# A hybrid layer's mixers reordered: a head's inputs prepared while its neighbour runs, the first phase's products in another order

## The reference

```python
proj = rmsnorm(x, norm_gain) @ w_in
# A, 6 heads: q, f_logit, i, gate, 128 columns each
log_f = logaddexp(log(lb), log1p(-lb) + log_sigmoid(z)); k = (1 - lb) * sigmoid(-z)
q = silu(q) * 128 ** -0.5                       # linear recurrence with decay exp(cumsum(log_f))
ya = rms(o) * hgrn_gain * silu(gate)
# B, 5 heads: attention over the own 64-row chunk and the 8 before it, bias by clipped distance
yb = softmax(q k^T / sqrt(128) + bias) v * silu(gate)
# C, 5 heads, 64 columns for q and for k: rotary, then retention with gamma_h = 1 - 2^(-5-h)
yc = rms(o) * silu(gate)
out = rmsnorm(x + concat(ya, yb, yc) @ w_out, final_gain)
```

## Time and profile before

| | |
|---|---|
| median of 3 runs | 2023.78 us (2017.93 to 2024.95) |
| the profiled execution's own time | 2020.91 us |
| its span, first to last instruction | 2019.1 us |
| TensorE busy | 1820.4 us (90%), 8758 matmuls |
| VectorE, ScalarE, GpSimd busy | 1247.6, 669.0, 694.4 us |
| mean granted clock of TensorE | 0.957 |
| phase 1, phase 2, phase 3 begin | 9.0, 608.8, 1677.2 us |

### The profile page before, as it was taken

How to read it: one execution, slowest core, us unless ns; L and a number is a source line. 1 busy time by engine, 2 the same in 40 slices (tenths; PEclk the granted TensorE clock), 3 DMA queues, 4 the chain that set the end, 5 groups by cost and what they waited for, 6 DMA issues and landing times.

```text
span 2019.1 us, 23727 instructions
## 1 busy us (share of the span) xinstructions
PE 1820.4 (90%) x8758; PEld 1497.3 (74%) x8758; DVE 1247.6 (62%) x1764; ACT 669.0 (33%) x974; POOL 694.4 (34%) x485
## 2 busy tenths in 40 slices
PE   6999999999986979879797899888988778999996
PEld 5888888888865868768686777777776666888875
DVE  5766756669676665756667144444544445877977
ACT  3333433333233333343334122222323322333442
POOL 3542001445434333433343332232322333045441
PEclk9999999999997989889898999999988889999998
DMA  6776535889873222222222322233322238777875
GB/s 220 229 238 194 168 120 177 285 269 367 304 262 118 84 63 74 84 79 89 71 76 68 117 86 78 75 101 102 102 85 81 69 95 292 249 239 241 286 246 218
DMA packets 160838, 323.08 MB, mean 160 GB/s; under 512 B 18378, under 2 KB 19151, under 8 KB 160724
## 3 DMA queue, kind: packets, MB, share of 16 engines
q1 hardware_dynamic: 146458, 276.52, 42.0%
q10 hardware_dynamic: 14266, 45.05, 6.5%
HBM read 275.35 MB, written 46.15 MB: 159 GB/s over the span
## 4 chain that ended last, share of the span: by engine, by line
PE 52%; DVE 7%; ACT 4%; issue 3%; DMA 3%; SPq 1%; POOL 0%; ACTq 0%; DVEq 0%; POOLq 0%
PE prj L762 29%; PE prj L1048 11%; PE mix L825 2%; ACT arena L1089 2%; PE mix L781 2%; PE mix L897 2%; PE mix L880 1%; DMA y_in<-y_scratch 1%; ACT arena L1092 1%; DVE arena L2060 1%; DMA x_even<-in_xT 1%; PE mix L890 1%; PE mix L792 1%; PE mix L852 1%; DMA in_raw<-in_wi 1%
## 5 line engine op out<-in xcount | busy, mean ns | idle before, releaser
L714 POOL TENSOR_SCALAR w_hi<-w_sum 128x512 fp32r<-128x512 f32 x124 | 203.2, 1639 | 718.5 <-DMA w_sum<-in_w 674.9
L741 PE MATMUL prj<-in_hi,w_hi 128*128 128x512 f32 x840 | 330.6, 394 | 22.9 <-DVE w_lo L1569 15.5
L708 POOL TENSOR_TENSOR w_sum<-in_raw,in_raw 128x512 f32<-128x512 f32 x150 | 206.6, 1379 | 389.1 <-PE prj L741 328.8
L741 PE MATMUL prj<-in_hi,w_lo 128*128 128x512 f32 x840 | 328.2, 391 | 0.0
L741 PE MATMUL prj<-in_lo,w_hi 128*128 128x512 f32 x840 | 328.1, 391 | 0.0
L762 PE MATMUL prj<-mv_hi,w_hi 128*128 128x512 f32 x928 | 310.8, 417 | 16.7 <-DVE land_pad L1963 11.4
L762 PE MATMUL prj<-mv_lo,w_hi 128*128 128x512 f32 x928 | 294.7, 399 | 0.0
L762 PE MATMUL prj<-mv_hi,w_lo 128*128 128x512 f32 x928 | 291.0, 395 | 0.0
L762 PEld LDWEIGHTS prj<-mv_lo,w_hi 128*128 128x128 f32 x928 | 181.0, 195 | 40.8
L762 PEld LDWEIGHTS prj<-mv_hi,w_lo 128*128 128x128 f32 x928 | 177.9, 192 | 39.9
L762 PEld LDWEIGHTS prj<-mv_hi,w_hi 128*128 128x128 f32 x928 | 171.9, 197 | 47.9 <-DVE land_pad L1963 11.8
(11 more groups left out here) (175 smaller groups left out, 2515.5 us busy)
## 6 DMA issues: line engine op xcount, KB each, us to landing
in_raw<-in_wi SPq DMA_DIRECT2D x360, 256.0 KB, 3.8
raws<-in_wo SPq DMA_DIRECT2D x184, 256.0 KB, 3.6
w_sum<-in_w SPq DMA_DIRECT2D x116, 256.0 KB, 3.1
arena<-z_scratch ACTq DMA_DIRECT2D x56, 512.0 KB, 3.4
y_in<-y_scratch SPq DMA_DIRECT2D x80, 256.0 KB, 4.6
z_scratch<-acc_in SPq DMA_DIRECT2D x60, 256.0 KB, 4.8
z_scratch<-stage SPq DMA_DIRECT2D x26, 512.0 KB, 4.1
x_even<-in_xT SPq DMA_DIRECT2D x44, 256.0 KB, 4.1
```

The costliest lines, as they stand in the source:

```text
L708: nc.gpsimd.tensor_tensor(w_sum[wslot(n)][:], in_raw_buf(a), in_raw_buf(b), ALU.add if sign > 0 else ALU.subtract).then_inc(in_wsum, 1)
L714: nc.gpsimd.tensor_scalar(w_hi[q][:], w_sum[q][:], 1.0, None, ALU.mult).then_inc(w_hi_done, 1)
L741: last = nc.tensor.matmul(out, wt[wslot(n)][:, i % GRAN, :], mv[j % 2][:, i, :], start=(i == 0 and wt is w_hi and mv is in_hi), stop=(i == ...
```

## The change

Phase 1 runs its products in the order M2, M5, M1, M6, M7, M3, M4, so that the two with one weight term come last; for these (granules from IN_ONE = 150) GpSimd writes w_lo in place of VectorE. All 60 tiles' halves are complete only in the last two products, and are scaled and stored in pairs, six steps later (five before). Squares are taken beside other products, and at the start after the first eight granules' weights. h's rows begin one step earlier, the last two in swapped order. The rows of arena are renamed so that head 0 of A is prepared during the last product. A's slots begin at -4 (A_FROM), B's at 121, C's at 183, 192, 201, 210; the last C head's output product moves to slot 229, inside the projection, one of its sums of squares to slot 231.

```diff
-A_EACH, B_EACH, C_EACH = 20, 12, 9
-B_FROM, C_FROM, C_LAST = 127, 187, 2 * NG * (STD - 1)
+A_FROM, A_EACH, B_FROM, B_EACH = -4, 20, 121, 12
+C_AT = [183, 192, 201, 210]
-IN_PRODUCTS = [M2, M5, M4, M3, M1, M6, M7]
+IN_PRODUCTS = [M2, M5, M1, M6, M7, M3, M4]
...
+            pool.wait_ge(w_split, IN_ONE)
+            for n in range(IN_ONE, IN_GRANULES):
+                m = in_raw_of[n][0]
+                pool.wait_ge(in_w_hi, n + 1)
+                nc.gpsimd.tensor_tensor(w_lo[wslot(n)][:], in_raw_buf(m), w_hi[wslot(n)][:].bitcast(F32),
+                                        ALU.subtract).then_inc(w_split, 1)
...
-                put(b + 24, a_ss(u, 0))
-                put(b + 25, a_ss(u, 1))
+                put(b + 22, a_ss(u, 0))
+                put(b + 24, a_ss(u, 1))
...
+                put(b, c_ktr(i), c_vtr(i))
+                put(b + 1, c_scores(i))
+                put(b + 2, c_state(i))
+                put(b + 4, c_out(i))
+                put(b + 5, c_ss(i, 0))
+                put(b + 6, c_ss(i, 1))
+            for slot_at, part in ((223, c_ktr), (224, c_scores), (225, c_vtr), (227, c_state), (229, c_out)):
+                put(slot_at, part(last_c))
+            put(231, c_ss(last_c, 0))
```

In the last product, after the steps named (v counts from its first): the loads of head 0 (4, ScalarE), a_head(0) (7, VectorE), the decay's and the silu's passes on ScalarE (8 to 10), a_logf, a_key, a_scan (10 to 12), the first differences (13), Q*K at the end. Of the mixers the new orders, ScalarE's head of A, VectorE's, and C's on both:

```diff
+            def a_unit(u):
+                b = A_FROM + A_EACH * u
+                if u > 0:
+                    a_z_first(u)
+                    a_z_second(u)
+                    sigmoid(2 * u, Q)
+                    norm_first(0, A_M0 * u, 2 * u, u - 1)
+                    kd_exp_of(u)
+                    qe_exp_of(u)
+                    lv_exp_of(u, 0)
+                    norm_second(2 * u)
+                    norm_ln(1, A_M1 * u, 16 * u)
                 act.wait_ge(diag_prod, u + 1)
                 part_high(arr(SC)[:, 0:HALF])
+                if u > 0:
+                    norm_exp(1, A_M1 * u)
+                else:
+                    h_high(15)
...
+                if u > 0:
+                    a_logf(u)
+                    a_key(u)
+                    a_scan(u)
+                    kd_diff_of(u)
+                    part_low(arr(T2)[:, 0:HALF], A_PARTS * u - 2)
+                    lv_diff_of(u, 0)
+                    a_diag_prod(u)
+                    part_low(arr(T2)[:, HALF:SEQ], A_PARTS * u - 1)
+                    lv_diff_of(u, 1)
+                    qe_mult(u)
+                    part_low(arr(SC)[:, 0:HALF], A_PARTS * u)
+                    kd_mult(u)
+                    lv_mult(u, 0)
+                    a_finish_out(u - 1)
...
+                near_drain(u)
+                if u < A_HEADS - 1:
+                    a_head(u + 1)
+                dve.wait_ge(end_ready, u + 1)
...
+                    act.wait_ge(filled[1], M1_C + C_M1 * i + 2)
+                    act.wait_ge(c_qd, i + 1)
                     load_z(TC + 3 * i + 3, CQK, z0_in)
+                act.wait_ge(drained[0], M0_C + C_M0 * i + 2)
+                act.dma_start(dec, dec_d[i + 1]).then_inc(cdec_in, 16)
+                evict_until(b + 2)
+                if not late:
+                    load_z(TC + 3 * i + 4, VT, z2_in)
+                    partner(i + 1)
+                else:
+                    sigmoid(m)
+                norm_first(1, M1_C + C_M1 * i + 3, m + 1, A_HEADS + i)
...
+                key_scores(i)
+                if not late:
+                    landed(g + 3, CQK, z0_in, A_HEADS + B_HEADS + i + 2).then_inc(cq_ready, 1)
+                c_states(i)
...
+                    rotate(i + 1)
+                    silu_finish(m, GATE, 1.0)
+                    c_part_low(i, 0)
+                    landed(g + 4, VT, z2_in, A_HEADS + B_HEADS + i + 2).then_inc(v_ready, 1)
+                    c_part_low(i, 1)
+                    q_decay(i + 1)
+                scale_y(C0 + i, A_HEADS + i, m + 1, 1, M1_C + C_M1 * i + 3, 1.0)
```

More of the change, by code:

```diff
@@ L240, in in_acc @@
         def in_acc(p, c):
-            rows = U_ROWS if c in (C12, C21) else V_ROWS
-            return acc_in[:, rows[p], half(c[1])]
+            rows = U_ROWS if c in (C12, C22) else V_ROWS
+            return acc_in[:, rows[p], half(c[0])]
         def slot(mv, j, i):
@@ L1038, in _ @@
                 project(g, stages[first:first + 2 * NG])
-            c_out(C_HEADS - 1)()
             def product(n, s, rows):
@@ L1295, in a_mix @@
+                act.wait_ge(first_part_used, 2 * u + 1)
+                part_high(arr(SC)[:, HALF:SEQ])
+                evict_until(b + 6)
+                for n in range(2, NM):
+                    lv_exp_of(u, n)
+                    evict_until(b + (8, 9, 11, 12)[n - 2])
+                    if n == 2 and u > 0:
+                        store_y(u - 1)
                 sigmoid(2 * u + 1)
@@ L1859, in scale_y @@
                 tt(arr(Y), arr(Y), arr(GATE), ALU.mult).then_inc(y_ready, 1)
[L1861 to L1874 removed]
+            def scale_y(u, m, gate, n, o_drain, scale):
+                rms_y(u, m, n, scale)
+                gate_y(gate, n, o_drain)
@@ new lines, in _ @@
+            dve.wait_ge(gain_in, 16)
+            first_lo_of(0)
+            in_w_low(0)
+            first_lo_of(1)
+            first_lo_of(2)
+            in_w_low(1)
+            first_lo_of(3)
+            in_w_low(2)
+            in_w_low(3)
+            for i in range(4, HK):
+                first_lo_of(i)
+                in_w_low(i)
+            for v in range(IN_STEPS):
+                for idx in in_comb_at(v):
+                    in_comb_add(idx)
+                    if in_square_of(idx) is not None:
+                        in_add_square(in_square_of(idx))
+                for n in (2 * v + 4, 2 * v + 5):
+                    if 2 * OPEN <= n < IN_ONE:
+                        in_w_low(n)
+                for idx in in_comb_at(v):
+                    in_comb_low(idx)
+                if v == 6 * IN_PAIRS + 4:
+                    tables()
+                if v == 6 * IN_PAIRS + 6:
+                    bounds()
+                if 1 <= v < OPEN:
+                    for q in range(3 * v - 3, min(3 * v, HK)):
+                        in_add_square(q)
+                in_accumulate(v)
+                for k, sp_of in enumerate(spills):
+                    if sp_of[0] == v:
+                        in_scale(k)
+                if v in h_at:
+                    h_low(h_at[v])
+                if v == 6 * IN_PAIRS + 7:
+                    dve.wait_ge(start_dve, 6)
+                    a_head(0)
+                if v == 6 * IN_PAIRS + 10:
+                    a_logf(0)
+                if v == 6 * IN_PAIRS + 11:
+                    a_key(0)
+                if v == 6 * IN_PAIRS + 12:
+                    a_scan(0)
+                if v == 6 * IN_PAIRS + 13:
+                    kd_diff_of(0)
+                    lv_diff_of(0, 0)
@@ L1877, in b_block @@
+            a_diag_prod(0)
+            dve.wait_ge(w_split, IN_GRANULES)
+            nc.vector.tensor_copy(rstd[:], mix[1][:]).then_inc(rstd_ready, 1)
+            h_low(13)
+            h_low(14)
+            for u in range(A_HEADS):
+                a_unit(u)
             def b_block(i, p):
@@ L1924, in b_unit @@
                 tt(arr(Y), arr(Y), arr(GATE), ALU.mult).then_inc(y_ready, 1)
-            b_unit(0, first=True)
-            for i in range(1, B_HEADS):
+            landed(TB + 2, VT, z2_in, A_HEADS + 1).then_inc(v_ready, 1)
+            b_qk(0)
+            part_low(arr(T2)[:, 0:HALF], PARTS_C - 2)
+            part_low(arr(T2)[:, HALF:SEQ], PARTS_C - 1)
+            b_mask(0)
+            a_finish_out(A_HEADS - 1)
+            for i in range(B_HEADS):
                 b_unit(i)
```

673 lines of the change are left out of this document (340 added, 333 removed).

## The result

The changed kernel takes 1916.79 us (median of 4 runs, 1914.81 to 1920.46) against 2024.32 (2017.93 to 2024.95): 0.948 of the time before, 95% interval 0.945 to 0.950. The forecast was 1866 with a range of 1838 to 1906: the sign is right, the gain is 107.5 where 158 was forecast, and the time lies 11 us outside the range. The profiled execution took 1914.81 us, its span 1913.0.

What follows compares the result with a forecast made beforehand. TensorE was taken as the bound, with its idle time and lost clock to be won. Six parts' gains of 156.5 us from the profiled 2020.9 gave 1864, stated as 1866, range 1838 to 1906.

Steps and rivals of the forecast that it cites:

- part 3: Phase 1: lower halves 4 to 7 before squares, -7.5 us; one-term products last with two raw loads a step, -6.
- part 2: Head 0 of A prepared in phase 1's last product: 7 of 24.7 us remain, -17.5.
- Rival (e): Phase 1's last 30 steps paced by load, ScalarE, GpSimd in a row: slower than before, 2034 us; chance 0.02.
- Part 1: Group A: heads 1 to 5 lose their wait before the sum of squares of Q*K, -63.5 us.
- Part 4: Group B: V and the next q and k come earlier, so transposes stop waiting except 1.3 us; -35.
- Part 5: Group C: 53 us go, new waits of 5.6 in heads 0 to 2 and 5.9 in head 4; -22.
- Part 6: Start of phase 3: the 4.7 us for the last tile's eviction goes, fourth open granule 6.5 late; -5.
- Rival (d): GpSimd's lower halves cost VectorE up to 1.1 us each in the last product: 1888 us; chance 0.1.
- (b): Group C hides its rotation after all: 1839 to 1845 us; chance 0.15.
- (c): Group A keeps part of its wait, 4 us left a head: 1902 us; chance 0.2.

Runs made afterwards that it cites:

- experiment 1: On the changed kernel, SP's x loads for the last product's activations queued one step earlier: 1877.5 us; two steps earlier: 1877.9 us.
- experiment 3: On top of experiment 1 (one step earlier), x's rows for h in the last product also asked for one step earlier: 1864.6 us, ratio 0.923.
- experiment 7: On experiment 3, fourth open weight's load put ahead of the 16 raw-weight and y loads: 1872.0 us; instead y's loads behind the last open weight: 1861.9 us.
- experiment 4: On experiment 3, VectorE makes all of phase 1's lower halves and GpSimd none: 1866.0 us, ratio 0.923.
- experiment 5: On experiment 3, silu finished before the next head's rotation in C: 1852.5 us; with the lower half taken inside the rotation: 1847.6 us.
- experiment 8: On experiment 3, the second sum of squares in A's heads moved one slot later, 25 for 24: 1871.6 us, ratio 0.926.

## Why the prediction was wrong where it was, and right elsewhere

**The step that failed is part 3**, "the products of one term come last, with two raw loads a step in place of four: of the 7.2 us -6". It counted the loads and did not walk SP's queue with them: that a raw buffer is now freed by GpSimd's lower half in place of its sum, what x load stands behind the raw loads, and who waits for it. Measured, the ring costs 39.3 us by experiment 1. The second ring, 12.9 us by experiment 3, lies in the last product: part 2 called that product covered, with VectorE busy 70 of 81.6 us, and asked when x lands for its last row only. The small waits late in the first phase, of which part 3 had counted 6 as gained, are gone once the rings are open: from 400 us on TensorE waits only 1.2 us, at the phase's very end.

**Rival (e) was the nearest mechanism** ("phase 1's last 30 steps are paced by load, ScalarE, GpSimd in a row"), with 0.02. Its sign, lower halves from GpSimd ending TensorE's waits, did not show: the profile puts these waits to "issue". I priced it over 30 steps as if it had to eat the whole gain, and so kept it out of the range. It needed x's load as its fourth member, held for eight steps fully and for the last product in part, and lengthened each of the eight steps by 5.2 us as a mean, near the 5.6 that I had called necessary. Walked through with what was known it comes to 9.2 us a step or more: 1.3 on ScalarE (x, then the first w_hi), 2.6 for two lower halves, 1.9 for the four issues up to the end of x's, a landing of 3.4. That was to be had before the run; in the turn shown it is 10.3, since the landing takes 4.6.

**Part 1 held.** Heads 1 to 5 of A have no wait, one head takes 72.8 us (73 forecast), and TensorE is busy 443.0 of 450 us at a clock of 0.99. The margins in its head 1 are 2.1 and 2.6 us, 2.7 and 1.7 by the prediction.

**Part 2**: head 0 waits 6.6 + 0.5 where I had 3 and 2.4, which with their clock were to be 7. VectorE's last updates ended 5.2 us into phase 2, where I had 2.9, since head 0's own operations stood ahead of them. Of the operations behind them two took 2.2 and 2.3 us, where I had the short value for each. So slot 2 was later, and little was left to wait for at slot 4. The wait is 6.5 in experiment 3 too, so it is not the rings'.

**Part 4**: 1.0 at the first transposes (1.3 forecast), and ten waits of 5.3 in all before the transposes of B's probabilities (L907), for the copy of an output block into Y (L2016) that still fills their bank: one of 2.0 in the first head, five of 0.5 and four of 0.2. The kernel before had nine of the short ones, 3.2 us in all; only the first is new, and I had not seen it.

**Part 5**: three waits of 5.4, 4.9 and 4.9 (5.6 each), one of 6.0 before the last scores (5.9). The rows before the first of them show the order as described: rotation, silu, and then only ScalarE's square.

```profile
1387.08 1.23 DVE L2078 TENSOR_TENSOR arena<-arena 128x1024 f32<-128x1024 f32 x1 [5.86 <-ACT arena L1457]
1388.22 1.63 DVE L2079 TENSOR_TENSOR arena<-arena 128x1024 f32<-128x1024 f32 x1
1389.89 2.21 DVE L2082 TENSOR_TENSOR arena<-arena 128x1024 f32<-128x1024 f32 x1
1392.02 1.21 DVE L1622 SCALAR_TENSOR_TENSOR arena<-arena 128x1024 f32<-128x1024 f32 x1
...
1393.27 1.02 ACT L1377 ACTIVATE arena<-mix 128x1024 f32<-128x1024 f32 x1 [6.22 <-DVE arena L1622]
```

**Part 6**: the wait at the fourth open granule is 5.0 (6.5), and phase 3 is shorter by 4.7 (5). Its cause as I put it, the place behind 16 loads, holds for that granule: it landed 10.5 us after it was asked for, and in experiment 7, with nothing ahead of it, after 2.6, and its wait went. What failed there was the remedy. The 4.7 are not firm: in experiment 3 phase 3 is 341.3, 0.5 shorter than before.

**Rival (d)**, GpSimd's cost to VectorE, is there at 0.32 us an operation, but did not decide in experiment 4; **(b) and (c)** did not come about.

## What to carry to other kernels

When work that frees a buffer goes to another engine, write down the ring that this buffer closes (who waits for the load, what stands behind it on that engine, what that frees, and what load stands behind on the queue), add up one turn, and divide by the number of steps that it serves. Here one place in a queue decided whether a turn of some 10 us serves one step or two, 39 us of the whole. TensorE's waits that the profile gives to "issue", at nearly even distances (10.2 to 11.7 us) and with the other engines idle for most of the turn, were its mark here.

## What was not expected of the hardware

Here a low clock had a price only where TensorE set the pace. In the first ring, 25.6 of the 39 us are waits and some 13 are matmuls at a lower granted clock (0.82 as the mean of the stretch), but the ring set the pace there: at full clock the waits would have been longer by as much (an estimate, from a turn of 10.7 us and 5.45 for a step). Where TensorE did set it, the price shows. In experiment 5 the waits of its line fell by 12.3 us and the time by 17.0; in experiment 8 one wait grew by 2.7 us, and the matmuls behind it took 3.3 longer.

The fourth open weight, 256 KB, took 2.6 us to land with nothing ahead of it and 10.5 (1521.1 to 1531.6) with sixteen loads ahead of it, at some 390 GB/s. To put it first made the kernel slower even so, since its slot was not free and SP held the others back for it.
